# The first expert's rows found by a 0/1 slot table, and outputs pre-filled with the last norm's shift

## The reference, cut to what matters

```
x = LN1(alpha*x + mix)
logits = x @ router_w + router_b ; top 4 of 32 experts, gates = softmax over the 4
for each row and each of its experts e:
    h = x @ w_in[e] + b_in[e]            # 1024 -> 2048, gate and up halves
    a = min(g,7) * sigmoid(1.702*min(g,7)) * (clip(u,-7,7) + 1)
    y[row] += gate * (a @ w_out[e] + b_out[e])
out = (z - mean(z)) * rsqrt(var(z) + eps) * ln2_g + ln2_b ,  z = alpha*x + y
```

## Time and profile before

| | |
|---|---|
| three runs, us | 1349.28, 1344.98, 1348.16 (median 1348.16) |
| the profiled execution, us | 1353.49, span 1351.7 |
| busy: PE, DVE, ACT, POOL | 88%, 38%, 20%, 18% of the span |
| granted PE clock, mean | 0.949 of full speed |
| moved | 463.19 MB, mean 343 GB/s |
| chain that ended last | PE 51%, DMA 22%, issue 3%, DVE 2% |

### The profile page before, as it was taken

The page is one execution under the profiler, slowest core; times in us unless marked ns, Lnnn a source line. Parts: engine busy times, 40 slices in busy tenths (PEclk is TensorE's granted clock), DMA queues, the critical chain, the costliest instruction groups (busy, mean ns, idle before and its releaser), DMA issues.

```text
span 1351.7 us, 34179 instructions
## 1 busy us (share of the span) xinstructions
PE 1183.2 (88%) x12540; PEld 523.4 (39%) x12541; DVE 515.8 (38%) x875; ACT 272.8 (20%) x533; POOL 244.5 (18%) x214
## 2 busy tenths in 40 slices
PE   7998999937899999998899989989898989999760
PEld 6886545512233333432233423332333332533210
DVE  2996637764232222232223232420423320432226
ACT  0003233410102230141121211130121211131213
POOL 4000001331111221142120311221121212120113
PEclk9998899958999999999999999999999999999765
DMA  9702831549999999999999999999999999999963
GB/s 358 199 3 85 295 152 34 231 147 410 415 419 412 409 413 410 417 391 414 417 410 415 410 412 413 383 406 416 416 408 414 410 419 371 390 406 419 412 218 129
DMA packets 79977, 463.19 MB, mean 343 GB/s; under 512 B 12324, under 2 KB 20873, under 8 KB 29709
## 3 DMA queue, kind: packets, MB, share of 16 engines
q1 hardware_dynamic: 69083, 438.76, 80.2%
q0 software_dynamic: 8768, 17.47, 5.1%
q10 hardware_dynamic: 2066, 6.32, 1.2%
HBM read 447.51 MB, written 19.48 MB: 345 GB/s over the span
## 4 chain that ended last, share of the span: by engine, by line
PE 51%; DMA 22%; issue 3%; DVE 2%; ACT 0%; SPq 0%; DVEq 0%; ACTq 0%; POOLq 0%; POOL 0%
PE pu L1865 32%; PE rest L1879 17%; DMA ring<-in_e_in 13%; DMA ring<-in_e_out 8%; PE pu L1859 1%; PE rest L1890 1%; DVE fin L2081 0%; DVE bn L2063 0%; DVE xgT L2002 0%; DVE mv L2074 0%; DMA fin<-acc_rows 0%; DMA acc_rows<-y,row 0%; PE rest L1884 0%; SPq L281 0%; DMA xq<-x_rows,idx 0%
## 5 line engine op out<-in xcount | busy, mean ns | idle before, releaser
L1865 PE MATMUL pu<-ring,xgT 128*32 128x512 f32 x5248 | 587.9, 601 | 35.9 <-DMA ring<-in_e_in 35.2
L1865 PEld LDWEIGHTS pu<-ring,xgT 128*32 128x32 f32 x5248 | 161.8, 111 | 444.1 <-issue 443.3
L1879 PE MATMUL rest<-ring,hid 128*32 128x256 f32 x5248 | 302.2, 388 | 23.8 <-DMA ring<-in_e_out 16.3
L2032 DVE TENSOR_SCALAR gg<-pu 128x1280 f32<-128x1280 f32 x32 | 47.7, 1492 | 604.6 <-PE pu L1865 604.6
L1789 POOL DMA_INDIRECT acc_rows<-y,row x82 | 110.7, 1350 | 747.7 <-ACT y L1945 731.5
L1879 PEld LDWEIGHTS rest<-ring,hid 128*32 128x32 f32 x5248 | 168.7, 112 | 147.6 <-issue 46.1
L1945 ACT ACTIVATE y<-rest,gate 32x256 f32 x328 | 152.8, 466 | 297.1 <-issue 293.4
L1925 ACT ACTIVATE ss<-gg 128x1280 f32<-128x1280 f32 x32 | 40.7, 1272 | 537.7 <-DVE gg L2032 537.7
L866 PE MATMUL pair<-xt,ring 128*128 128x260 f32 x448 | 101.2, 388 | 7.3 <-DMA ring<-in_w_in 5.6
L1779 POOL DMA_INDIRECT xq<-x_rows,idx x82 | 88.2, 1075 | 91.9 <-issue 80.0
L866 PEld LDWEIGHTS pair<-xt,ring 128*128 128x128 f32 x448 | 86.2, 193 | 21.2 <-DMA xt<-in_xT 7.4
(11 more groups left out here) (270 smaller groups left out, 547.7 us busy)
## 6 DMA issues: line engine op xcount, KB each, us to landing
ring<-in_e_in SPq DMA_DIRECT2D x256, 1024.0 KB, 24.2
ring<-in_e_out SPq DMA_DIRECT2D x128, 1024.0 KB, 25.5
ring<-in_w_in SPq DMA_DIRECT2D x3, 1536.0 KB, 24.7
ring<-in_w_in SPq DMA_DIRECT2D x5, 512.0 KB, 11.0
ring<-in_w_o SPq DMA_DIRECT2D x1, 2048.0 KB, 12.0
conv<-in_x_prompt SPq DMA_DIRECT2D x1, 2048.0 KB, 13.8
x_rows<-conv ACTq DMA_DIRECT2D x4, 512.0 KB
acc_rows<-conv ACTq DMA_DIRECT2D x4, 512.0 KB
```

The source lines that it names most:

```text
L1865: mm = nc.tensor.matmul(pu[quarter(c), j], xgT[:, j, k], w[:, :, c * QC:(c + 1) * QC], start=False, stop=k == KT - 1, skip_group_check=True)
L1879: mm = nc.tensor.matmul(py[quarter(c), j], hid[:, j, 2 * q + f], w[:, f, c * QC:(c + 1) * QC], start=False, stop=q == FT // 2 - 1 and f == ...
L2032: V.tensor_scalar(gg[:, :, :], pu[:, :, 0], SW_LIMIT, None, ALU.min).then_inc(g_ready, 1)
```

## The change

Eight things change.

1. **A slot table for expert 0.** For each tile, DVE forms a 128x160 table of 0 and 1 in bfloat16: row r has its 1 in the slot equal to its rank + 1 if it belongs to expert 0 (`first_slots`, two DVE instructions). PE multiplies the table with the rows' numbers (`first_ids_of`: for 5 groups x tiles x 4 quarters, one matmul of two columns), which gives each slot's row number. Four tiles are done in one go, 80 matmuls, ahead of the last tile's logits; the last tile adds 20. DVE sums both parts into the gather's index table `idx4[:, 0]`, and counts expert 0's groups (`first_size`).
2. **The first gather moves into the first block.** POOL issues it as soon as the indices are there and all `x_rows` writes have landed. These are now counted on `x1_sent`, the `acc_rows` writes apart on `sums_begun`. The last tile's four list scatters, which stood ahead of it, move behind it into the second block.
3. **The job table moves** from the first block into the second, behind the first gather's turn on DVE. PE's part of it (`turn_fields`, 4 matmuls) stands in the middle of the first `up`. The next job's expert is found early as `next_expert`, so SP can load weights without the job table.
4. **The lists are loaded by ACT alone**, in the second block, behind the last scatters.
5. **Units 7 and 8** of expert 0 are loaded at the head of the second block.
6. **The row buffers** `xq`, `xgT` and `hid` share the memory of `qkv`, so that the gather can start in the first block; the clearing of `xq` by ACT and POOL goes.
7. **The PSUM banks** are shared by both blocks and cleared by DVE at the very start, not in the second block.
8. **Outputs.** After the bias rows are in place, POOL fills `y_prompt` and `y_sample` with `ln2_b` by five DMAs. At the end POOL adds each tile (norm times `ln2_g`) to the output with an adding indirect DMA of up to 128 rows; the adds of `ln2_b` on POOL and DVE, its load into SBUF and SP's output writes go.

```diff
+            def first_ids_of(tiles, dst):
+                pe.wait_ge(slots_ready, NTH[tiles[-1]])
+                for j in range(JG):
+                    for i in tiles:
+                        m = rows(i)
+                        for c in range(NQ):
+                            mm = nc.tensor.matmul(dst[c * GS:(c + 1) * GS, j], in_slot[0:m, i, j * GS:(j + 1) * GS],
+                                                  id_parts[0:m, i], start=i == tiles[0], stop=i == tiles[-1],
...
+            def first_slots(i, ranks):
...
+                ch.do(V.scalar_tensor_tensor(keys[0:m, i:i + 1], ranks[:, 0:1], 1.0, memb[0:m, i, 0:1], ALU.add, ALU.mult))
+                V.tensor_scalar(in_slot[0:m, i], C("slot", m), keys[0:m, i:i + 1], None, ALU.is_equal
+                                ).then_inc(slots_ready, 1)
...
+            d.wait_ge(ids_done, 1)
+            V.tensor_copy(early_ids[:, :, :], ids_early).then_inc(ids_kept, 1)
             root1(0)
...
+            gp.wait_ge(bias_rows, 2 + 16 * 6 * NQ)
+            shift_row = o["ln2_b"].partition_broadcast(P)
+            for i in range(NT):
+                gp.dma_start(o["y_prompt"][0, i * P:(i + 1) * P], shift_row).then_inc(y_begun, 16)
...
-            for i in (NT,) + TILES:
+            for i in (NT,) + TILES[:-1]:
                 list_rows(i, NTH[i])
+            gp.wait_ge(x1_sent, 16 * (NT + 1))
+            gp.wait_ge(first_named, 1)
+            size = gp.value_load(first_size[0:1, 0:1], min_val=1, max_val=JG)
...
+                gp.wait_ge(scaled2, n + 1)
+                nc.gpsimd.indirect_dma_start(
+                    out=dst, out_offset=bass.IndirectOffsetOnAxis(ap=out_rows[0:m, i % NT:i % NT + 1], axis=0),
+                    in_=fin[0:m, i], in_offset=None, compute_op=ALU.add,
```

More of the change, by code:

```diff
@@ L469, in first_block @@
         x1_sent = bsem("x1_sent")
+        sums_begun = bsem("sums_begun")
         q_sent = bsem("sample_queries_sent")
@@ new lines, in _ @@
+            ch.mark(V.scalar_tensor_tensor(key, totals, float(NE), C("tie", NE), ALU.mult, ALU.add))
+            ch.mark(V.tensor_copy(own[:, 2:3], total_column))
+            ch.do(V.scalar_tensor_tensor(mine, total_column, float(NE), C("tie1", NE), ALU.mult, ALU.add))
+            ch.do(V.tensor_scalar(beats, key, mine, None, ALU.is_gt))
+            ch.do(V.tensor_reduce(better, beats, AX.X, ALU.add))
+            ch.mark(V.tensor_scalar(placed[:, 0], C("place", NE), better, own[:, 2:3], ALU.is_equal, ALU.mult))
@@ L1793, in scatter @@
                 each_group(groups, rows_of)
+            for k in range(TOPK):
+                nc.gpsimd.indirect_dma_start(
+                    out=lists_dram.rearrange("s q c -> (s q) c"),
+                    out_offset=bass.IndirectOffsetOnAxis(ap=spots[:, 0, k:k + 1], axis=0),
+                    in_=pairs[:, 0, k], in_offset=None,
+                    bounds_check=GS * NE * MAXQ - 1, oob_is_err=False).then_inc(listed, 16)
             gp.sem_inc(y_free, 3)
[L1796 removed]
+            gp.wait_ge(jobs_ready, 1)
+            for u in range(1, 4):
                 size = size_of(slice(u, u + 1))
                 gp.wait_ge(named, u + 1)
[L1799 to L1807 removed]
+                done = before(slice(u, u + 1))
+                gp.wait_ge(gathered, 16 * done)
+                gp.sem_inc(gathers, 1)
                 if u >= 2:
@@ L1853, in each_group, with up @@
                 return f(j)
-            def up(groups, step):
+            def up(groups, step, between=None):
                 def bias(j):
@@ L1871, in up @@
                     each_group(groups, lambda j: unit(k, j)).then_inc(up_done, 1)
+                    if between and k == KT // 2 - 1:
+                        between()
             def down(groups, step):
@@ L1895, in down, with turn_fields @@
                     each_group(groups, lambda j: unit(q, j)).then_inc(down_done, 1)
+            def turn_fields():
+                pe.wait_ge(fields_ready, 1)
+                for k in range(3):
+                    nc.tensor.matmul(turned_fields[:, k * P:(k + 1) * P], fields[:, k:k + 1], C("ident"),
+                                     start=True, stop=True)
+                nc.tensor.matmul(turned_fields[:, 3 * P:4 * P], fields[:, 0:1], C("tri"), start=True, stop=True
+                                 ).then_inc(fields_turned, 1)
+            size = pe.value_load(first_size[0:1, 0:1], min_val=1, max_val=JG)
+            pe.wait_ge(turned, 1)
+            pe.wait_ge(chosen_ready, 1)
+            pe.wait_ge(pu_read, 1)
+            up(size, 1, turn_fields)
+            pe.wait_ge(jobs_ready, 1)
             last = job_count(pe)
@@ L2055, in _ @@
             fc = Chain(d, sem("ln2_chain"))
-            d.wait_ge(ln2_in, 32)
+            for i in range(NT):
+                V.tensor_scalar(out_rows[:, i:i + 1], C("job"), float(i * P), None, ALU.add).then_inc(out_named, 1)
+            d.wait_ge(ln2_in, 16)
             def moments(n):
```

380 lines of the change are left out of this document (211 added, 169 removed).

## The result

The changed kernel takes 1356.34 us (median of 4 runs, 1354.82 to 1357.02), the kernel before 1348.17 beside it: ratio 1.0053, with a 95% interval of 1.0036 to 1.0069. It is 8 us slower, where 10 us less was forecast.

The account below looks back on a forecast made before the run. The prediction took the experts' weight stream, by its start and bytes, and the stretch after the last scatter as the bound; -8.3 and -1.5 gave -9.8, so 1338.4 us from the 1348.16 median, own range 1334.5 to 1342, wider range 1333 to 1345.5.

Parts of the forecast that it names:

- nothing is late, by 2 us: Behind the first job: job table near 301, second gather landed near 307, rows turnable near 309, 2 us to spare.
- the sum: The forecast's total: 8.3 us off the stream's end, 0.3 for added bytes included, and 1.5 off the end: -9.8.
- rival 4: PE's second job: job table and gather come 6 us late, the early start is lost; 1347 us, chance 0.08.
- The first stretch: From the last tile's turn to the first expert job: PE starts 8.6 us earlier (6.5 to 10.0), at 288.7.
- T: Start of DVE's last routing in the first block, forecast at 274.5 us (273.1 to 276.6), 3.5 later than before.
- The end: From the last scatter to the span's end: worked out as 1.8 us earlier, taken as 1.5.
- Rival 3: At the end the output adds become the bound, 7.8 us a tile: 1358.4 us in all, chance 0.06.

Follow-up runs that it names:

- hold_stream: Changed kernel, where SP starts reloading the ring only once DVE has named the rows of the first three jobs; 1354.95 us, ratio to before 1.0051.
- one_copy2: Changed kernel with one copy of the up products, in PE's loop, whose first pass has a single step; 1351.05 us, ratio to before 1.0017.
- peeled_before: Kernel before, with a second copy of the up products for its first job, ahead of the loop; 1357.59 us, ratio 1.0070.
- sp_waits: Changed kernel, where SP and not POOL waits at the very end for the adding DMAs to land; 1352.46 us, ratio to before 1.0029.

## Why the prediction was wrong

1. **"So the experts' stage is a stream of weights, and its end hangs on when the stream starts and on how many bytes pass."** This is the step that failed. It was read from full DMA slices. But a full slice says that the ring is being refilled, not who waits: the waits of PE and the busy time by window, which were there before, say that PE paces the fourth to the tenth job. A stream that starts sooner only fills the ring sooner and stops; behind that it is as late as PE is. hold_stream shows it: the stream 10 us later, the time the same.
2. **"...nothing is late, by 2 us."** The table was ready at 299.6 as forecast (301), but the names at 304.6 to 306.9 waited for the lists, whose 640 KB stood in the sum as 0.3 us of bytes and not as a wait; the gather behind them took 6 us under the full stream where the earlier trace rows had 2.62; the second job started at 316.0, some 5 us later than its rows were to be ready. This is rival 4, given a chance of 0.08 with the lateness put at 6 us. But its time, 1347, held no loss beyond the lead.
3. **A step that was missing.** That `up` now stands twice in PE's program was to be read in the kernel, and no term stood for it. one_copy2 and peeled_before price it at 7 and 9 us in the second job. The Trainium skill (Runtime: NRT & Kernel Launch, "Instruction fetch mechanics") has an engine's program come in blocks of 16 KiB through a DMA queue of its own, a crossing "mostly hidden" and a taken branch out of the window a stall. The trace agrees on the blocks and the queue (q8); hidden they are not here, with 7.8 us of stalls in the second job.
4. **The first stretch came out right, in part by luck**: first job 8.0 us earlier counted from the slots (forecast 8.6), the reload 4.0 behind it (4.7). The `x_rows` write was the last thing that the gather waited for, as forecast: in the trace its semaphore is full at 276.49, 1.0 us behind the indices (275.45), and the second of the gather's two DMAs landed at 282.38, T + 11.8 (forecast T + 11.7). But two errors cancelled. The 80 matmuls took 1.48 us, not 4.0, and T came 2.2 us sooner than worked out. And the gather did not land last: POOL's drain at the block's end, for which the sum had nothing, ran from 278.98 to 283.70 and held all engines. DVE moved again at 284.41 and turned the rows at 285.41, T + 14.9 in place of T + 11.7.
5. **The end: the term was mis-sized**, 3.7 us more in place of 1.5 less. DVE's products were right, and so, in the main, was the price per row: most of the 520 packets of 4 KB took 0.328 us (forecast 0.33), but some up to 1.1, and 58.0% of 16 engines x 21.3 us over all 520 are 0.38 each. Counted from the last scatter, the last packet came 2.2 later than worked out, with POOL's issues at 1.53 to 2.03 us for 1.32. The greater part is the tail: 0.8 us from the last packet to the end was taken from SP's write, and behind POOL's adds it is 4.1, with the drain in it that the sum left out here too. Rival 3 had the sign, by a wrong cause: a tile's adds did not take 7.8 us.
6. The Trainium skill (SBUF — State Buffer, "SBUF: two separate sides") lets a DVE instruction with two SBUF inputs block GpSimd only in an operation that reads SBUF. The prediction took from it that a POOL issue costs no more beside such a product; but these issues take their rows from a table in SBUF (`out_rows`), so the rule does not settle it. The issue at 1338.87, beside two products, took 2.03 us, the one at 1335.86, beside one in its last 0.6 us, 1.57, the last two, beside none, 1.53. That one issue was 0.5 us longer; no run isolates why.

## What to carry to other kernels

Before a lead is counted as a gain, ask at the next point where two engines meet which of them waits: full DMA engines do not show that the weights are the bound. A transfer or a piece of program that was free while the DMA engines were idle has to be priced again when the change starts the stream ahead of it. And the end of a block has to be priced with the drain of the engine that is last there, which should not be the one that also waits for the output: here POOL's drain held the start of the experts' block and the end of the kernel.

## What the runs showed of the hardware

- PE's program comes over the DMA engines in pieces of 16 KB; under a stream of 404 GB/s they are 5.7 to 6.3 us apart, PE goes on 1.4 to 1.5 us behind each, and a loop that has run once fetches nothing more (no packet on q8 after 344.6 us in the changed kernel).
- POOL's drain at a block's end lasts until after its DMAs have landed: 1.7 us past the landing when it was already waiting (sp_waits), and 3.3 us in all when it started after it (after). With no DMA of POOL's under way it ended 3.2 us behind POOL's last add (before, 1346.30 to 1349.49).
- An adding DMA to the output moves a row of 4 KB in 0.328 us of one engine (median); the plain write's packets of that size took 0.16 in the trace of before.
